# w_out's rows for the attention output in transfers over 128 partitions in place of two over 64

## What is computed

```python
def mix_out(o_nsa, o_pool, w_out):
    B, T = o_pool.shape[:2]
    return jnp.concatenate([o_nsa.reshape(B, T, NSA_W), o_pool], axis=-1) @ w_out
...
    q, kvc_p, kvs_p, kvw_p, gates, u_p = mix_inputs(h, w_in, g_qnorm, g_knorm)
    o_nsa = nsa_prompt(q, gates, kvc_p, kvs_p, kvw_p, cmp_pe, w_cmp, g_knorm, slopes)
    o_pool = pool_mix(u_p, jnp.zeros((Bp, POOL_BUF, POOL_W), u_p.dtype), jnp.arange(Tp), w_pool, pool_scale)
    x1 = x_prompt + mod_p[:, 2][:, None, :] * mix_out(o_nsa, o_pool, w_out)
    h2 = modulate(x1, mod_p[:, 3], mod_p[:, 4], g_norm2)
    y_prompt = x1 + mod_p[:, 5][:, None, :] * peer(h2, peer_wq, peer_subkeys, peer_u, peer_v)
```

## Time and profile before

| | |
|---|---|
| median of 3 runs | 2570.46 us (2568.68 to 2578.82) |
| the profiled execution | 2574.56 us, of it 2572.8 us span |
| VectorE busy | 1757.6 us (68%) |
| TensorE busy | 1280.7 us (50%) |
| GpSimd busy | 1184.3 us (46%) |
| moved by DMA | 944.49 MB, 367 GB/s on average |
| granted TensorE clock, mean share | 0.699 |

### The profile page before, as it was taken

One profiled execution on the slowest core, in us unless ns is written; L12 is line 12 of the kernel. 1 busy time (PEld: TensorE's weight loads), 2 busy tenths in 40 slices (PEclk: granted clock), 3 DMA queues, 4 the chain that ended last, 5 costly groups with the idle time before them and its releaser, 6 DMA issues.

```text
span 2572.8 us, 17754 instructions
## 1 busy us (share of the span) xinstructions
PE 1280.7 (50%) x6315; PEld 697.2 (27%) x6317; DVE 1757.6 (68%) x2243; ACT 212.5 (8%) x559; POOL 1184.3 (46%) x686
## 2 busy tenths in 40 slices
PE   5699998897490543266884972000015655200000
PEld 2363534482240432143331960000002222000000
DVE  1010112217967977897557667999999998899898
ACT  3110012100001221121001010000000000000000
POOL 1000100002426744575222415678876767788684
PEclk9799898899795655556995985555556677655555
DMA  9949899659999999999998989999999999999897
GB/s 299 332 172 422 324 414 291 208 196 360 388 422 397 377 366 341 405 410 370 344 373 321 414 318 410 366 393 422 422 407 407 400 420 417 417 422 422 366 422 307
DMA packets 163042, 944.49 MB, mean 367 GB/s; under 512 B 34635, under 2 KB 44435, under 8 KB 56830
## 3 DMA queue, kind: packets, MB, share of 16 engines
q0 software_dynamic: 94784, 682.66, 66.0%
q1 hardware_dynamic: 68175, 260.74, 28.2%
HBM read 937.36 MB, written 10.26 MB: 368 GB/s over the span
## 4 chain that ended last, share of the span: by engine, by line
PE 27%; DMA 25%; DVE 20%; POOL 15%; issue 9%; SPq 2%; ACT 1%; POOLq 0%; another core or an unknown queue 0%; DVEq 0%; ACTq 0%
POOL arena L668 11%; DMA arena<-in_peer_u,arena 10%; DMA arena<-in_peer_v,arena 9%; DVE arena L1975 8%; POOL arena L680 4%; DVE arena L1998 4%; DMA arena<-in_w_out 4%; PE PS L1468 3%; PE PS L1445 3%; PE PS L1016 3%; DMA arena<-in_w_ada 3%; PE PS L1166 2%; PE PS L1253 2%; PE PS L966 2%; PE PS L1423 2%
## 5 line engine op out<-in xcount | busy, mean ns | idle before, releaser
L668 POOL DMA_INDIRECT arena<-in_peer_u,arena x256 | 471.7, 1843 | 446.1 <-DVE arena L1975 240.8
L1975 DVE CUSTOM_DVE_ANT_0 arena<-arena 128x2048 f32<-128x2048 f32 x256 | 581.5, 2289 | 118.0 <-DMA arena<-in_peer_u,arena 116.7
L1998 DVE SCALAR_TENSOR_TENSOR arena<-arena 128x2048 f32<-128x2048 f32 x226 | 531.1, 2350 | 136.6 <-DMA arena<-in_peer_v,arena 131.9
L668 POOL DMA_INDIRECT arena<-in_peer_v,arena x256 | 428.3, 1673 | 369.7 <-DVE arena L1998 242.7
L1468 PE MATMUL PS<-arena 128*128 128x512 f32 x240 | 180.3, 921 | 449.9 <-DMA arena<-in_peer_v,arena 449.9
L1468 PEld LDWEIGHTS PS<-arena 128*128 128x128 f32 x240 | 69.5, 304 | 561.4 <-issue 555.1
L1474 PE MATMUL PS<-arena 128*64 128x512 f32 x8 | 5.5, 849 | 346.4 <-DVEq L2041 346.4
L2031 DVE SCALAR_TENSOR_TENSOR arena<-arena 128x2048 f32<-128x2048 f32 x64 | 150.6, 2352 | 10.8 <-DMA arena<-in_peer_v,arena 5.3
L966 PE MATMUL PS<-arena 128*32 128x512 f32 x768 | 119.4, 721 | 69.9 <-DMA arena<-in_w_ada 66.6
L2028 DVE CUSTOM_DVE_ANT_0 arena<-arena 128x2048 f32<-128x2048 f32 x64 | 145.0, 2291 | 8.4 <-DMA arena<-in_peer_u,arena 6.5
L680 POOL DMA_INDIRECT arena<-in_peer_v,arena x64 | 126.4, 1975 | 39.0 <-issue 18.6
(11 more groups left out here) (347 smaller groups left out, 1824.5 us busy)
## 6 DMA issues: line engine op xcount, KB each, us to landing
arena<-in_w_ada SPq DMA_DIRECT2D x96, 1024.0 KB, 12.1
arena<-in_w_in SPq DMA_DIRECT2D x32, 1048.0 KB, 9.2
arena<-in_peer_wq SPq DMA_DIRECT2D x32, 1024.0 KB, 10.2
arena<-in_w_in SPq DMA_DIRECT2D x32, 768.0 KB, 11.2
arena<-in_w_out SPq DMA_DIRECT2D x16, 1024.0 KB, 30.0
arena<-in_w_out SPq DMA_DIRECT2D x32, 512.0 KB, 24.0
arena<-in_peer_u,arena POOLq DMA_INDIRECT x320, 13.9
arena<-in_peer_v,arena POOLq DMA_INDIRECT x320, 15.5
```

The source lines that it names most:

```text
L668: pool.indirect_dma_start(out=rows_ring[:, k % NROW, :], out_offset=None, in_=tables[kind], in_offset=bass.IndirectOffsetOnAxis(ap=ids[:, ...
L1975: V.tensor_tensor_reduce(out=buf, in0=buf, in1=h2(t), scale=1.0, scalar=0.0, op0=ALU.mult, op1=ALU.add, accum_out=dots[:, t, r:r + 1]).the ...
L1998: V.scalar_tensor_tensor(out=acc[t], in0=rows_ring[:, k % NROW, :], scalar=dots[:, t, r:r + 1], in1=acc[t], op0=ALU.mult, op1=ALU.add).the ...
```

## The change

The attention pieces are issued over all 128 partitions. For tile 0 the loop over gi goes, and the source is the view with both gi in it: `[gi = 2, d = 64, n = 2048]`, 2 blocks of 64 rows, the blocks 256 rows apart. One transfer takes the place of two, so the piece adds 16 to its semaphore and not 32. For tiles 1 and 2 there are still two transfers to a piece, but each now takes one chunk over 128 partitions (source `[2, 64, 1024]`) and not both chunks over 64. Bytes, order of pieces, slots and everything that reads them stay.

```diff
-            count[k % 12] += 32 if p[0] == "out" and p[1] < 8 or p[0] == "out1" and p[2] < 4 else 16
+            count[k % 12] += 32 if p[0] == "out1" and p[2] < 4 else 16
...
             elif kind == "out":
-                for gi in range(2):
-                    eng.dma_start(dst[64 * gi:64 * gi + 64, 0:D], w_out_nsa[n // 4, gi, :, n % 4, :]).then_inc(done, 16)
+                eng.dma_start(dst[:, 0:D], w_out_nsa[n // 4, :, :, n % 4, :]).then_inc(done, 16)
...
                 if c < 4:
-                    for gi in range(2):
-                        eng.dma_start(pair[64 * gi:64 * gi + 64], w_out_nsa[c // 2, gi, :, 2 * (c % 2):2 * (c % 2) + 2, cols]).then_inc(done, 16)
+                    for i in range(2):
+                        eng.dma_start(pair[:, i, :], w_out_nsa[c // 2, :, :, 2 * (c % 2) + i, cols]).then_inc(done, 16)
```

## The result

The changed kernel takes **2867.57 us** (median of 4 runs, 2863.15 to 2871.32), the kernel before 2569.57 us (2562.43 to 2578.82). The ratio is 1.116, 95% interval 1.1143 to 1.1176: slower by 298 us, where +213 us (2784 us) was predicted. The profiled execution of after has a span of 2869.5 us, 296.7 more than the 2572.8 of before.

What follows compares the result with a forecast made beforehand. DMA was taken to bound most of the span from the first gather on, TensorE tile 0's projection. 98 + 30 + 83 + 2 = +213 us on the profiled 2574.6, less 4 for the median: 2784 us; range 2700 to 2890.

Steps and rivals of the forecast that it cites:

- Two engines: Every merged attention transfer: source's outermost size 2 gives two engines, 20.0 us a piece in place of 6.5.
- Rival A: Attention transfers spread over all 16 engines; tile 0 gains nothing, later pieces gain 34 us: 2537 us; chance 0.09.
- rival B: Attention transfers use 16 engines but go through 64 partitions at a time, at the old rate: 2570 us; chance 0.05.
- Rival C: Two engines, but tiles 1 and 2 hide most; tile 0's 98 us and a third of 113 remain: 2706 us; 0.08.
- Rival D: Tiles 1 and 2: beside gathers w_out gets a third of the two engines' time, 60 us a piece: 2860 us; 0.10.
- Tile 0: +98 predicted: Tile 0's output projection: two engines need 180 us from 401 us, so it ends at 585 us, not 487.4.
- Early pieces: +30 predicted: Tiles 1 and 2's two early attention pieces, ahead of the value pages: 27 us added work, a few for later pages.
- I count the engines' added work: 27: Early pieces of tiles 1 and 2: 40 us on the two engines in place of 13, as DMA was busy throughout.
- Projection: +83 predicted: Tiles 1 and 2's other six attention pieces: add1(1) can run at 1458 us against 1375 before.
- TensorE takes 3.6 us for a piece: Tiles 1 and 2's projection: with loads of 2.5 us, the last pooling products add some 10 us.
- the 245 us: Each of two engines, from 1198 us: six attention pieces 120, pooling pieces 20, x inputs 5, 40 gathers 100.
- Clock: 2 us taken: Tile 0's last piece: lower TensorE clock could make 8 products take 7 us; 0 to 10 us in all, 2 taken.

Runs made afterwards that it cites:

- e4: The changed kernel with attention transfers reading 4 blocks of 32 rows, 256 rows apart (other rows of w_out): 2705.78 us, +136.
- e3: The changed kernel with attention transfers reading 16 blocks of 8 rows, 64 rows apart (other rows of w_out): 2564.87 us, ratio 0.9985.
- e10: The changed kernel with every attention transfer reading 128 neighbouring rows in plain form (wrong rows): 2539.48 us, ratio 0.9888.
- e2: The kernel before with the new form for tiles 1 and 2 alone, tile 0 in its old form: 2751.93 us, +182.
- e7: The changed kernel with the two early attention pieces of tiles 1 and 2 in the old form of two 64-partition transfers: 2821.26 us.
- e9: The changed kernel with attention transfers reading 16 blocks of 8 rows, one every 9 rows (other rows of w_out): 2563.68 us beside 2570.49.
- e5: The kernel before with the gi = 1 halves of six out1 attention pieces issued from ScalarE's queue: 2569.1 us, ratio 1.0.

## Why the prediction was right in kind and short in size

**The mechanism held.** Two engines, read from L661's row as a rule of the outermost dimension, was the step that decided the case, and the rows of after, e4 and e3 show it for 2, 4 and 16. Rival A (16 engines) and rival B (the old rate) are out: share 0.13. Rival A's price of 34 us was sound, e10 gave 29. Rival C (tiles 1 and 2 hide most) is out: e2 alone costs 182 us.

**Rival D is there in part, and the measured time lies nearer to its 2860 us than to the forecast's 2784.** Its mechanism, w_out getting a third of an engine's time while gathers are in flight, can be read from after. The queues in 1480 to 1510 us, where no gather is in flight, then in 1530 to 1590 us, beside gathers (packets, MB, share of 16 engines; q1 has SP's loads, q0 the gathers):

```profile
q1 hardware_dynamic: 389, 1.56, 12.8%
...
q0 software_dynamic: 2345, 17.04, 81.2%
q1 hardware_dynamic: 254, 1.03, 4.6%
```

1.56 MB in 30 us is 52 GB/s, 1.03 MB in 60 us is 17 GB/s: a third, one piece in 60 us. At the early pieces D's price was paid in full (see below). At the projection it wasn't: VectorE stood 76 us at add1(0) and 78 us at add1(1), not the 5 us at add1(0) of the sum, no gathers were issued meanwhile, and the last attention piece was used 271 us after the first product, not 360. The range held the measured time because it was drawn to take in D; the sum by itself missed by 84 us.

**Tile 0: +98 predicted, +114 measured.** The first attention piece was used at 427.61 (predicted landing 423.5), a step took 23.5 us for 22.5, and the last piece came 27.7 us after the one before it, not 20. From 560 to 590 us, while the `peer_wq` pieces behind it run on the other engines, the DMA share is 0.60 to 1.05, and 0.12 to 0.13 on either side of that; that they slow the last piece is likely, but no run tested it. That this place had no other cover, and that TensorE's wait would be some 100 us, was right: its eight waits add up to 98.1 us. The trace has no landing times for the L431 transfers, for which 60 us was named; for the pooling pieces between them it is 47.5 us in the median. SP didn't stand eight pieces ahead: it was held in its issues.

**Early pieces: +30 predicted, +48 measured.** The failed step is "I count the engines' added work: 27". The work added isn't the cost, but how long the two engines take for it beside gathers, since the value pages stand behind it. w_out's 512 packets of 4 KB run from 1121.6 to 1240.9 us in after (from 1008.4 to 1033.2 in before), 119 us for two pieces where D had 120, and TensorE goes on at 1243.13 us. SP's 65.33 us in issuing four transfers, with the pages of all samples issued behind, fit the same backlog. e7 took back 46 us.

**Projection: +83 predicted, +132 measured.** The step that failed most is "TensorE takes 3.6 us for a piece". That is a piece of tile 0, 8 products; an out1 piece serves two tiles of tokens and has 16. The earlier trace rows had it all along: x80, five pieces, 37.53 us, 7.5 us each. So the tail is 37 us and not 10, some 27 of the 49 missing. The 40 gathers of the sum were 40:

```profile
L667 POOL DMA_INDIRECT arena<-in_peer_v,arena x40: 932/936/2929, 1360.0 to 1590.7; - x40
```

A second part is that the 245 us were made with packets at full speed. In the trace's packet records an 8 KB packet of a gather takes a mean of 322 ns in after while gathers run alone (700 to 1000 us), and 377 ns beside w_out's packets (1500 to 1590 and 1370 to 1430 us), the mean of all 16 engines. An engine carries 8 such packets of a gather: 40 x 8 x 0.055 = 18 us. The 4 KB packets of w_out take 173 to 181 ns there, 159 at the least: six pieces put 768 of them on an engine, 11 to 17 us. Together this would cover the other 22 us, but no run isolated it, so it stays an estimate. It isn't the price of sharing an engine as such: from 1198 to 1350 us, at a share of 1.02 both times, the two kinds of packet take 316 and 162 ns in e10, where w_out comes in plain pieces, and 383 and 193 ns in before. e4, with four engines, lost 49 us in the same stretch.

**Clock: 2 us taken.** The last product of tile 0 took 5.19 us and not 3.6, at a mean granted clock of 0.72 from 596 to 602 us: 1.6 us. TensorE had stood idle for 22.34 us before it, and the clock was at 0.50 from 580 us on.

**What stays open.** Why 16 blocks of 8 rows, and the old halves, move at 15 to 17 GB/s for each engine where plain rows reach 26. The distance in HBM is out (e9), the two halves taking turns is out (e5), and the engines' number is out (e3). Nor is it the form of the source by itself: alone in flight, 8 KB packets of the two-block form take 310 ns (440 to 448 us in after) and of the four-block form 336 ns (439 to 445 us in e4), against 315 ns for the whole pieces of 350 to 380 us in before, and means of 510 and 477 ns at e3's and e9's tile 0. And it slows others, as the gathers' 383 ns beside the old halves show. Which partitions the engines write at the same moment is a candidate that no run tested.

## What to carry to other kernels

Before two transfers are merged into one, read off the outermost size of the merged source: blocks that lie apart make it the number of blocks, and here that was the number of engines, so 2 blocks took 8 times as long per piece on the engines concerned as an even spread would. A transfer on few engines isn't only slow itself (and here three times slower again beside gathers): whatever else must use these engines is late, and so is all that stands behind it in the issuing engine's queue, so the queue's other users belong in the sum. Where rows lie badly for a load that is repeated or urgent, copying them once within HBM while the DMA engines have room, and then loading them in one plain transfer, was worth 23 us here for the load on the path, while the copies moved the first gather by 1 us.

## What the runs showed of the hardware

- The number of engines follows the outermost size of the source even where the destination has 128 partitions: 2 blocks, share 0.13 and 53 GB/s; 4 blocks, 0.26 and 100 GB/s; 16 blocks, 1.02.
- A transfer over all 128 partitions on all 16 engines isn't thereby at full rate: 260 and 278 GB/s with 16 blocks at tile 0 at a share of 1.02, while plain rows gave 283 GB/s at a share of 0.76 (408 and 416 later on).
- Issuing isn't free when few engines serve: an out1 attention issue that took 0.6 us in the median held SP for 10.3 us in the median and 36.3 at most, and a plain issue between such ones 19.9 us for 0.33. It fits that SP waits for room in the queues of the two engines, since e7, with the old form for four issues, has 2.74 us for them; what the limit is wasn't measured.
- Two queues on the same two engines: w_out's 4 KB packets moved 52 GB/s with no gather in flight and 17 GB/s beside gathers' 8 KB packets.
- Sharing engines with gathers slowed nothing when both came in plain form (e10: 316 and 162 ns for 8 and 4 KB packets at a share of 1.02); beside 64-partition transfers they took 383 and 193 ns (before).
- Two 64-partition halves issued from two queues gain nothing over one queue (ratio 1.0).
